# Stick-breaking attention in a hybrid block: heads paired in the array, meta keys of four heads in one tile, bonus rows parked in memory, new orders of steps

## The chip, the cores and the metric

One core of a Trainium2 chip runs the whole kernel. The metric is the device time of one execution in microseconds. The engines are TensorE (PE in the profile), VectorE (DVE), ScalarE (ACT), GpSimd (POOL) and SyncE (SP, which here only starts transfers). Each works through its own list of instructions in order and waits for the others on semaphores.

## The reference

A block on 16 learned meta tokens and 512 tokens, width 1024, float32: RMS norm, one input projection, then two branches side by side: stick-breaking attention with 8 heads of 64 and an RWKV-7 time mix with 8 heads of 64. Their outputs are projected, gated by sigmoids, added, projected again; a SwiGLU feed-forward of width 2816 follows. The attention of one head is what the change touches most:

```python
z = jnp.einsum('bhqd,bhsd->bhqs', q_blk, k).astype(jnp.float32) * (HEAD_DIM ** -0.5)
visible = jnp.arange(T)[None, :] < q_pos[:, None]
neg_log_1m_beta = jnp.where(visible, jax.nn.softplus(z), 0.0)
between = lax.cumsum(neg_log_1m_beta, axis=3, reverse=True) - neg_log_1m_beta
weights = jnp.where(visible, jnp.exp(jax.nn.log_sigmoid(z) - between), 0.0)
return jnp.einsum('bhqs,bhsd->bhqd', weights.astype(v.dtype), v)
...
bonus = jnp.sum(rh * kh * r_k.astype(f32), axis=-1, keepdims=True) * vh
y = (y + bonus.reshape(B, T, RW_WIDTH)) * g.astype(f32)
```

Only the rows of the 512 tokens leave the kernel, so only their queries are computed; keys are all 528.

## The kernel before, in words

The kernel has four stages. First the norm and 26 units of the input projection (a unit is 128 output columns; its weights are split in a high and a low half on ACT and DVE, `hi_unit` and `lo_unit`, and multiplied in three products of 8 steps each, L540). Then the **mixing stage**, with which this document deals. Then the rest of the gate units and the two branch projections, woven with the end of the time mix (`LATE`: squares, variance, gate, bonus, output). Last the output projection and the feed-forward.

In the mixing stage four kinds of work are woven into one list for each engine, written out by hand as text (`ORDER_PE`, `ORDER_ACT`, `ORDER_DVE`, `ORDER_POOL`). A token such as `a3.Q2` is a kind, a number and a step:

- `i0` to `i4`: the inverse of a triangular matrix for two chunks of 64 tokens each (steps A, L, then W, R, Y for five levels). A level goes from PE to ACT (`w`, `xt`), to PE, to DVE (`x`) and back.
- `s0` to `s8`: the recurrent state from chunk to chunk (F, RB, T0 to T2, Z, SA, OUT, S), each step handed to ACT or DVE (`z`, `sa`, `out`, `s`) and back. Both kinds are matmuls of 64x64 in the four quadrants of the array (L1389).
- `a0` to `a7`: a head of the attention. Keys lie along the partitions, so a head has four tiles of 128 keys with 512, 384, 256 and 128 visible queries and a fifth of the 16 meta keys with 512. `Q0` to `Q4` are the score products of these tiles (L1541): contraction 64, so half of the array's rows. `z0` to `z4` copy them out on ACT (L842), `m0` to `m3` mask the diagonal blocks on POOL. Softplus is `min`, `exp`, `ln(1+.)`, `max` over a row of 1792 numbers in two halves of 896. Its high and low halves (`hi`, `lo`) go through `C3` to `C0` and `C4`, products with triangles of ones that build the reversed sum in one bank (L1559, L1563), which `s3` to `s0` and `s4` subtract. `w1`, `w0`, `wm` take the exponential and `O` is the product with the values (L1576, L1578): 64 output columns, so half of the array's columns.
- `g0` to `g9`: ten gate units in four pieces of six matmuls each (L1426); `u0` is a further unit.

The score tiles of a head go to two banks by turns. The orders on ACT put the four exponentials and logarithms of a head together.

Of the kernel before, what the change touches and what calls it, by code (L numbers as in the profile page):

```python
# [28 lines left out]
F32 = mybir.dt.float32  # L29
# [26 lines left out]
N_ZERO = 3  # L56
# [10 lines left out]
K_ID, K_TRI, K_CTRI, K_BLK, K_LT, K_LE, K_IST, K_CEN, K_RST = 0, 128, 256, 384, 512, 576, 640, 704, 768  # L67
# [20 lines left out]
PIECES = 4  # L88
# [69 lines left out]
KINDS = {"i": "inv", "s": "seq", "a": "att", "g": "gate", "u": "unit"}  # L158
# [13 lines left out]
a0.Q0 a0.Q1 a0.Q2 a0.Q3 a0.Q4 i0.A i0.L a1.Q0 a1.Q1 g0.G0 i0.W1 i0.R0 a1.Q2 a1.Q3 g0.G1 g0.G2 a1.Q4 i0.Y1 a0.C3  # L172
g0.G3 a0.C2 s0.F s0.RB a0.C1 i0.W2 i0.R1 a0.C0 g1.G0 a0.C4 i0.Y2 s0.T0 s0.T1 s0.T2 g1.G1 a0.O a2.Q0 a2.Q1 a2.Q2
a2.Q3 a2.Q4 a1.C3 i0.W3 i0.R2 a1.C2 s0.Z g1.G2 a1.C1 i0.Y3 g1.G3 a1.C0 i0.W4 i0.R3 a1.C4 g2.G0 i0.Y4 g2.G1 a1.O
a3.Q0 a3.Q1 a3.Q2 a3.Q3 a2.C3 a3.Q4 i0.W5 a2.C2 i0.R4 a2.C1 g2.G2 a2.C0 i0.Y5 a2.C4 s0.SA i1.A s0.OUT s0.S i1.L
g2.G3 a2.O s1.F i1.W1 i1.R0 s1.RB a3.C3 a4.Q0 a4.Q1 a3.C2 i1.Y1 a4.Q2 a4.Q3 i1.W2 s1.T0 i1.R1 s1.T1 s1.T2 a3.C1
a4.Q4 a3.C0 i1.Y2 s1.Z1 s1.Z a3.C4 i1.W3 s1.SA i1.R2 s1.OUT1 s1.OUT s1.S i1.Y3 g3.G0 i1.W4 i1.R3 s2.F s2.RB a3.O
i1.Y4 s2.T0 s2.T1 s2.T2 g3.G1 i1.W5 i1.R4 s2.Z1 s2.Z a4.C3 g3.G2 i1.Y5 a4.C2 g3.G3 i2.A s2.SA i2.L a4.C1 s2.OUT1
s2.OUT i2.W1 s2.S i2.R0 a4.C0 g4.G0 i2.Y1 s3.F s3.RB a5.Q0 a5.Q1 i2.W2 i2.R1 s3.T1 s3.T0 s3.T2 a5.Q2 i2.Y2 a4.C4
g4.G1 g4.G2 i2.W3 i2.R2 s3.Z1 s3.Z a5.Q3 a5.Q4 i2.Y3 s3.SA g4.G3 i2.W4 i2.R3 s3.OUT1 s3.OUT s3.S a4.O i2.Y4 s4.F  # L180
s4.RB g5.G0 i2.W5 i2.R4 g5.G1 i2.Y5 s4.T1 s4.T0 s4.T2 a5.C3 i3.A i3.L a5.C2 g5.G2 i3.W1 i3.R0 s4.Z1 s4.Z a6.Q0
a6.Q1 i3.Y1 s4.SA a5.C1 i3.W2 i3.R1 s4.OUT1 s4.OUT s4.S i3.Y2 a5.C0 g5.G3 a5.C4 i3.W3 i3.R2 s5.F s5.RB a6.Q2
a6.Q3 i3.Y3 s5.T1 s5.T0 s5.T2 a6.Q4 i3.W4 i3.R3 s5.Z1 s5.Z g6.G0 g6.G1 i3.Y4 s5.SA g6.G2 i3.W5 i3.R4 s5.OUT1
s5.OUT s5.S i3.Y5 g6.G3 i4.A i4.L a5.O i4.W1 i4.R0 s6.F s6.RB g7.G0 i4.Y1 s6.T0 s6.T1 s6.T2 i4.W2 i4.R1 a6.C3
g7.G1 a6.C2 g7.G2 i4.Y2 s6.Z1 s6.Z i4.W3 i4.R2 s6.SA a7.Q0 a7.Q1 i4.Y3 a6.C1 i4.W4 i4.R3 s6.OUT1 a6.C0 i4.Y4
s6.OUT s6.S i4.W5 i4.R4 g7.G3 a6.C4 i4.Y5 s7.F a7.Q2 a7.Q3 g8.G0 a7.Q4 s7.RB g8.G1 g8.G2 g8.G3 s7.T0 s7.T1 s7.T2
g9.G0 g9.G1 s7.Z1 s7.Z a6.O s7.SA a7.C3 g9.G2 a7.C2 s7.OUT1 s7.OUT s7.S a7.C1 g9.G3 a7.C0 s8.F s8.RB a7.C4 u0.U
s8.T2 a7.O s8.Z1 s8.Z s8.SA s8.OUT1 s8.OUT
# [3 lines left out]
a0.z0 a0.z1 a0.z2 a0.z3 a0.z4 a0.exp1 a0.exp0 a1.z0 a1.z1 a0.ln1 a0.ln0 a1.z2 a1.z3 i0.xt0 i0.w1 a1.z4 g0.hi  # L192
a0.w1 i0.w2 i0.xt1 a0.w0 a0.wm a1.exp1 a1.exp0 a1.ln1 a1.ln0 a0.o a2.z0 s0.kh a2.z1 a2.z2 s0.bh a2.z3 a2.z4
i0.xt2 i0.w3 s0.z a1.w1 g1.hi a1.w0 i0.xt3 i0.w4 a2.exp1 a1.wm a2.exp0 a2.ln1 a2.ln0 a1.o a3.z0 a3.z1 a3.z2
a3.z3 a3.z4 i0.xt4 i0.w5 a2.w1 a2.w0 s0.sa a3.exp1 a3.exp0 a2.wm s0.out a3.ln1 a3.ln0 g2.hi a2.o i1.w1 i1.xt0
a4.z0 a4.z1 a4.z2 a4.z3 a3.w1 i1.w2 i1.xt1 s1.bh s1.kh a4.z4 a3.w0 s1.z s1.sa i1.w3 i1.xt2 a4.exp1 s1.out
a4.exp0 a3.wm a4.ln1 i1.xt3 i1.w4 a4.ln0 a3.o s2.bh s2.kh i1.xt4 i1.w5 s2.z a4.w1 s2.sa g3.hi s2.out i2.xt0
i2.w1 a4.w0 a5.z0 a5.z1 i2.xt1 i2.w2 s3.bh a5.z2 s3.kh a4.wm i2.xt2 i2.w3 a5.z3 s3.z a5.z4 s3.sa a5.exp1 a5.exp0
i2.xt3 i2.w4 s3.out g4.hi a5.ln1 a5.ln0 a4.o i2.w5 i2.xt4 s4.kh s4.bh a5.w1 i3.xt0 i3.w1 s4.z a6.z0 a6.z1 s4.sa
i3.xt1 i3.w2 s4.out a5.w0 g5.hi a5.wm i3.w3 i3.xt2 a6.z2 a6.z3 s5.kh s5.bh a6.z4 i3.w4 i3.xt3 a6.exp1 a6.exp0  # L200
s5.z a6.ln1 s5.sa a6.ln0 i3.xt4 i3.w5 s5.out g6.hi a5.o i4.xt0 i4.w1 s6.bh i4.xt1 i4.w2 s6.kh a6.w1 s6.z i4.w3
i4.xt2 s6.sa a7.z0 a7.z1 i4.xt3 i4.w4 a6.w0 s6.out i4.w5 i4.xt4 g7.hi a6.wm a7.z2 a7.z3 a7.z4 a7.exp1 a7.exp0
a7.ln1 s7.bh a7.ln0 s7.kh g8.hi s7.z a6.o s7.sa a7.w1 s7.out g9.hi a7.w0 a7.wm a7.o s8.z s8.sa s8.out
# [15 lines left out]
a7.lo0 g8.lo s7.decay a7.s3 a7.s2 a7.s1 s7.s g9.raw a7.s0 s8.ark s8.aak s8.arb a7.s4 g9.lo s8.v
# [22 lines left out]
def build(nc, x, meta, w_in, w_sb, w_rw, w_out, w_g, w_u, w_d, decay_up, aaa_up, gate_up,  # L242
          vecs, g_mix_pre, g_mix_post, g_ffn_pre, g_ffn_post, kf, kb, out):
    with ExitStack() as ctx:
# [34 lines left out]
        reset = consts[:, K_RST:K_RST + T]  # L279

# [14 lines left out]
        vmeta = sb("v_meta", [META, 512])  # L295
# [42 lines left out]
        cursor[0] = mix_at  # L338
# [18 lines left out]
        sp_hi = sb("softplus_hi", [P, NS], F32R)
        tri_r = sb("tri_r", [P, 2 * P], F32R)
# [92 lines left out]
        bonus_dve = sem("bonus_dve")  # L451
        tri_ok = sem("tri_ok")
# [107 lines left out]
        def y_of(p):  # L560

            return ar[:, 0, p, C:TP]


        @block.sync
        def _(sp):
# [9 lines left out]
            for dst, src in ((masks_f[:], kb), (consts[:, K_TRI:NK], kf[:, K_TRI:NK]), (lora[0:64, :], decay_up),  # L576
                             (lora[64:P, :], aaa_up), (gup[:], gate_up)):
                sp.dma_start(dst, src).then_inc(const_in, 16)
            for u in range(2, U_FFN):
                load_unit(sp, u)  # L580
                i = u - U_MIX - 4
                if 0 <= i < EARLY:
                    sp.wait_ge(mix_dve, upto(MIX_DVE, "gate", i, "raw"))
                    sp.dma_start(kept[i], gate_raw[i % 2][:]).then_inc(gate_kept[i % 2], 16)
                if u < U_OUT and MERGE[u - U_MIX][0] == "branch" and u >= U_MIX and MERGE[u - U_MIX][1] >= AHEAD:
                    j = MERGE[u - U_MIX][1]
                    if j == AHEAD:
                        for i in range(2):
# [1150 lines left out]
```

## Time and profile before

| | |
|---|---|
| time, median of 3 runs | 969.02 us (966.11 to 969.81) |
| profiled execution | 965.5 us, its span 963.7 us |
| PE busy | 921.8 us (96%) |
| DVE busy | 475.8 us (49%) |
| ACT busy | 400.8 us (42%) |
| POOL busy | 73.9 us (8%) |
| DMA | 81.17 MB, mean 84 GB/s |

The span is from the first to the last instruction; the profiled execution's own time is 1.8 us longer. Busy times are sums of instructions; matmuls are pipelined, so their busy times overlap, and what a matmul costs is read from the distance between the starts of neighbours.

### The profile page before, as it was taken

How to read it: one execution, taken by the hardware profiler on the slowest of the kernel's cores; microseconds unless marked ns; L12 is line 12 of the kernel's file. 1: busy time of each engine (PE TensorE's matmuls, PEld its weight loads, DVE VectorE, ACT ScalarE, POOL GpSimd, SP SyncE). 2: the span in 40 equal slices, each digit the busy share in tenths (PEclk: the TensorE clock that was granted, in tenths of full speed). 3: DMA queues.
4: the chain of work that ended last, by engine and by line, in shares of the span. 5: the costliest groups of instructions: out<-in, count | busy, mean ns of one | idle time of the engine just before them, and what ended most of it. 6: DMA issues, size and time to landing. Idle time of an engine off the chain costs nothing.

```text
span 963.7 us, 18924 instructions
## 1 busy us (share of the span) xinstructions
PE 921.8 (96%) x8205; PEld 739.0 (77%) x8205; DVE 475.8 (49%) x614; ACT 400.8 (42%) x576; POOL 73.9 (8%) x99
## 2 busy tenths in 40 slices
PE   4999999989999999998999996999999999999997
PEld 3999999856667677775678785888888888888886
DVE  5357876236576356362657562444444444422253
ACT  5344555356665546455444353232232232221241
POOL 1011112111111011101220000000000000000000
PEclk9999999979999999998999997999999999999999
DMA  8322212301110102121136631333332332323321
GB/s 259 103 80 81 87 50 84 88 23 35 34 35 27 42 7 69 35 66 46 45 88 220 242 84 43 87 98 98 100 96 87 90 106 87 104 93 92 105 83 70
DMA packets 108862, 81.17 MB, mean 84 GB/s; under 512 B 2878, under 2 KB 99432, under 8 KB 108792
## 3 DMA queue, kind: packets, MB, share of 16 engines
q1 hardware_dynamic: 108792, 80.13, 27.5%
q8 instruction: 57, 0.93, 0.4%
q14 instruction: 13, 0.11, 0.0%
HBM read 75.40 MB, written 4.72 MB: 83 GB/s over the span
## 4 chain that ended last, share of the span: by engine, by line
PE 92%; ACT 2%; DVE 2%; issue 2%; DMA 1%; POOL 1%; SPq 0%; POOLq 0%; DVEq 0%; ACTq 0%
PE psum L540 48%; PE psum L1624 17%; PE psum L1389 9%; PE psum L1426 6%; PE psum L1541 3%; PE psum L1578 2%; PE psum L1563 2%; PE psum L1559 1%; PE psum L1576 1%; PE psum L1310 1%; DMA x_in<-in_x 1%; ACT w_hi L525 1%; PE psum L1359 0%; PE psum L1355 0%; PE psum L1343 0%
## 5 line engine op out<-in xcount | busy, mean ns | idle before, releaser
L540 PE MATMUL psum<-h_hi,w_hi 128*128 128x512 f32 (+1 forms) x784 | 247.5, 352 | 4.8 <-DVE h_lo L998 1.7
L540 PE MATMUL psum<-h_lo,w_hi 128*128 128x512 f32 (+1 forms) x784 | 244.3, 348 | 0.0
L540 PE MATMUL psum<-h_hi,w_lo 128*128 128x512 f32 (+1 forms) x784 | 242.7, 346 | 0.0
L540 PEld LDWEIGHTS psum<-h_hi,w_hi 128*128 128x128 f32 x784 | 137.7, 190 | 27.7 <-issue 4.1
L540 PEld LDWEIGHTS psum<-h_lo,w_hi 128*128 128x128 f32 x784 | 137.0, 190 | 20.0 <-issue 1.2
L540 PEld LDWEIGHTS psum<-h_hi,w_lo 128*128 128x128 f32 x784 | 137.0, 190 | 18.7
L530 DVE TENSOR_TENSOR w_lo<-w_raw,w_hi 128x1024 fp32r<-128x1024 f32 x69 | 85.7, 1243 | 132.1 <-ACT w_hi L525 132.1
L1265 DVE TENSOR_TENSOR w_lo<-w_raw,w_hi 128x1024 fp32r<-128x1024 f32 x44 | 53.9, 1225 | 138.7 <-ACT w_hi L976 138.7
L525 ACT ACTIVATE w_hi<-w_raw 128x1024 fp32r<-128x1024 f32 x70 | 73.7, 1054 | 81.0 <-PE psum L1624 63.4
L976 ACT ACTIVATE w_hi<-w_raw 128x1024 fp32r<-128x1024 f32 x44 | 46.5, 1056 | 72.5 <-PE psum L540 72.5
L1624 PE MATMUL psum<-w_hi,act_hi 128*128 128x512 f32 x144 | 45.7, 389 | 0.0
L1624 PE MATMUL psum<-w_lo,act_hi 128*128 128x512 f32 x144 | 45.7, 389 | 0.0
L1624 PE MATMUL psum<-w_hi,act_lo 128*128 128x512 f32 x144 | 45.6, 389 | 0.0
L973 ACT ACT_TABLE_LOAD x11 | 14.1, 1283 | 54.8 <-PE psum L540 54.8
L1541 PE MATMUL psum<-qT,kT 64*128 64x512 f32 (+4 forms) x80 | 33.5, 532 | 3.3 <-DVE tri_r L1091 3.2
L1426 PE MATMUL psum<-h_hi,w_hi 128*128 128x512 f32 x80 | 34.5, 432 | 0.1
L973 ACT ACTIVATE ffn_t<-psum 128x512 f32<-128x512 f32 x22 | 13.2, 599 | 50.5 <-PE psum L540 50.4
L1112 DVE COPY_PREDICATED x_inv<-byte_masks,psum 128x512 f32<-128x512 uint8 (+1 forms) x25 | 16.9, 677 | 33.7 <-PE psum L1389 33.6
L1169 DVE TENSOR_TENSOR scores<-scores,psum 128x128 f32<-128x128 f32 (+4 forms) x40 | 20.9, 523 | 23.5 <-PE psum L1563 23.3
L1426 PE MATMUL psum<-h_lo,w_hi 128*128 128x512 f32 x80 | 32.1, 401 | 0.0
L1426 PE MATMUL psum<-h_hi,w_lo 128*128 128x512 f32 x80 | 32.1, 401 | 0.0
L1624 PEld LDWEIGHTS psum<-w_lo,act_hi 128*128 128x128 f32 x144 | 27.0, 188 | 5.7
(257 smaller groups left out, 1454.9 us busy)
## 6 DMA issues: line engine op xcount, KB each, us to landing
w_raw<-in_w_in SPq DMA_DIRECT2D x42, 512.0 KB, 3.8
w_raw<-in_w_g SPq DMA_DIRECT2D x22, 512.0 KB, 3.8
w_raw<-in_w_u SPq DMA_DIRECT2D x22, 512.0 KB, 3.8
w_raw<-in_w_d SPq DMA_DIRECT2D x22, 512.0 KB, 3.6
w_raw<-in_w_out SPq DMA_DIRECT2D x8, 512.0 KB, 5.5
kept_gates<-gate_raw SPq DMA_DIRECT2D x10, 256.0 KB, 2.3
sig_t<-kept_gates SPq DMA_DIRECT2D x10, 256.0 KB, 3.0
x_in<-in_x SPq DMA_DIRECT2D x4, 512.0 KB, 6.4
```

What stands on the lines that cost most here:

```text
L525: nc.scalar.activation(split(u)[0][:], raw[u % RAW][:], ACT.Copy).then_inc(w_hi_done, 1)
L530: nc.vector.tensor_sub(lo[:], raw[u % RAW][:], hi[:].bitcast(F32)).then_inc(w_split, 1)
L540: mm = nc.tensor.matmul(o, w[:, (w0 + i) * P:(w0 + i + 1) * P], xs[:, k, c0:c1], start=(n == 0), stop=(n == total - 1))
L973: s_.activation(ffn_t[t][:], bank(2 * t), ACT.Sigmoid).then_inc(f_sig, 1)
L976: s_.activation(w_hi[v % SPL][:], raw[v % RAW][:], ACT.Copy).then_inc(w_hi_done, 1)
L1169: v_.tensor_tensor(d, d, psum[0:rows, CBANK, SEQ - WIDTH[j]:SEQ], ALU.subtract).then_inc(mix_dve, 1)
L1265: v_.tensor_sub(w_lo[v % SPL][:], raw[v % RAW][:], w_hi[v % SPL][:].bitcast(F32)).then_inc(w_split, 1)
L1389: mm = t_.matmul(psum[rows(p, hd, moved), bnk + p // 2, o0:o0 + n], w(k, p), m(k, p), start=first, stop=last, skip_group_check=True)
L1426: mm = t_.matmul(bank(GBANK), w[:, k * P:(k + 1) * P], xs[:, k, META:T], start=(k == 0 and i == 0), stop=(k == KT - 1 and i == 2))
L1541: t_.matmul(psum[0:kn, QBANKS[j % 2], 0:WIDTH[j]], kT[lanes, hp, k0:k0 + kn], qT[lanes, hp, SEQ - WIDTH[j]:SEQ], start=True, stop=True).th ...
L1563: mm = t_.matmul(psum[0:kn, CBANK, SEQ - WIDTH[j]:SEQ], tri_r[0:kn, 0:kn], part[0:kn, OFF[j]:OFF[j] + WIDTH[j]], start=(j == 3 and part is ...
L1624: mm = t_.matmul(bank(2 * b + h), xs[:, k, P * b:P * b + P], w[:, 512 * h:512 * h + 512], start=(k == 0 and i == 0), stop=(k == n - 1 and ...
```

## The change

1. **Pairs of heads.** `a0` to `a3` are now pairs. `Q0`, `Q1`, `Q2` issue the products of both heads in turn, one on the upper and one on the lower 64 rows of the array, into a bank each; `Q2` holds the tiles of 256 and 128 queries, which share a bank. One ACT instruction `z` copies both banks. `O` issues the ten matmuls in turn for the two heads, one to the left and one to the right 64 columns. The softplus part stays by head, and is named `h0` to `h7`; its two parts are now 896 and 384 long instead of 896 and 896.
2. **Meta keys.** `m0` and `m1` hold the 16 meta keys of four heads each, at partitions 0, 32, 64 and 96 of one tile of 512 queries: two matmuls with 64 output columns each (`km` holds the keys, with zeros between), one `min`, `exp`, `ln`, `max`, `hi`, `lo` for four heads. `C4` multiplies this tile with a triangle by blocks of 32 (`K_TM`).
3. **Bonus rows.** To make room, the 1 MB of bonus rows is written to memory before the mixing stage (`kept_bonus`) and read back when `i4.x5` is done. ACT, DVE and POOL have tiles there and DVE and POOL wait for the write; POOL's addition in `LATE` waits for the read.
4. **Gate pieces.** A gate unit is two pieces of twelve matmuls (`PIECES = 2`).
5. **Orders.** All four lists are new. PE no longer waits for the copy `tri_r` ahead of the stage, only ahead of the first C.

```diff
-PIECES = 4
+PIECES = 2
...
+                if u == N_IN + 1:
+                    sp.wait_ge(bonus_dve, PAIRS)
+                    sp.dma_start(kept_bonus, bonus[:]).then_inc(bonus_kept, 16)
...
+                if i == EARLY:
+                    for k in range(2):
+                        sp.wait_ge(gate_kept[k], 16 * ((EARLY + 1 - k) // 2))
+                    sp.wait_ge(bonus_kept, 16)
+                    sp.wait_ge(mix_dve, upto(MIX_DVE, "inv", len(BATCHES) - 1, f"x{LEVELS - 1}"))
+                    sp.dma_start(bonus[:], kept_bonus).then_inc(bonus_back, 16)
...
-            pe.wait_ge(tri_ok, 1)
...
+                if kind == "att" and s[0] == "Q":
+
+                    j = int(s[1])
+                    if j == 2:
+                        if n < 2:
+                            pe.wait_ge(mix_act, upto(MIX_ACT, "meta", n, "z"))
                         else:
+                            pe.wait_ge(mix_act, upto(MIX_ACT, "att", n - 2, "o"))
+                    else:
+                        pe.wait_ge(mix_act, upto(MIX_ACT, "att", n, f"z{j + 1}"))
+                    for t in ((0,), (1,), (2, 3))[j]:
+                        k0, c0 = META + P * t, OFF[t] - OFF[j]
+                        for hr in range(2):
+                            mm = t_.matmul(psum[:, QBANKS[hr], c0:c0 + WIDTH[t]], kT[head(hr), n, k0:k0 + P],
+                                           qT[head(hr), n, SEQ - WIDTH[t]:SEQ], start=(t == j), stop=True,
+                                           skip_group_check=True)
+                    mm.then_inc(mix_pe, 1)
...
+                    for j in range(QB):
+                        for hr in range(2):
+                            v0 = (2 * n + hr) * HD
+                            mm = t_.matmul(psum[head(hr), QBANKS[1], SEQ - WIDTH[j]:SEQ], vtok[:, j, v0:v0 + HD],
+                                           zs[n % 2][:, hr, OFF[j]:OFF[j] + WIDTH[j]], start=False, stop=(j == QB - 1))
```

What the orders do is shown at three places. At the start of the mixing stage PE has, before, the five score products of head 0 one after the other (`qT,kT`, with the number of output partitions and of queries), then the first steps of the inverse (`a_r,b_t`, `b_t,a_r`):

```order
L1541 MATMUL psum<-qT,kT 128x512
L1541 MATMUL psum<-qT,kT 128x384
L1541 MATMUL psum<-qT,kT 128x256
L1541 MATMUL psum<-qT,kT 128x128
L1541 MATMUL psum<-qT,kT 16x512
L1389 MATMUL psum<-a_r,b_t 64x64 x16
L1389 MATMUL psum<-b_t,a_r 64x64 x16
L1541 MATMUL psum<-qT,kT 128x512
L1541 MATMUL psum<-qT,kT 128x384
```

and of change, where `k_meta` is the tile of meta keys:

```order
L1458 MATMUL psum<-a_r,b_t 64x64 x16
L1597 MATMUL psum<-qT,k_meta 64x512 x2
L1458 MATMUL psum<-b_t,a_r 64x64 x16
L1458 MATMUL psum<-a_r,k_t 64x128 x8
L1613 MATMUL psum<-qT,kT 128x256 x2
L1613 MATMUL psum<-qT,kT 128x128 x2
L1458 MATMUL psum<-a_r,b_t 64x64 x8
L1458 MATMUL psum<-x_inv,aab 64x64 x16
L1458 MATMUL psum<-consts,x_inv 64x64 x16
L1613 MATMUL psum<-qT,kT 128x384 x2
```

The first step of the inverse now stands ahead of all scores, and the score products come in twos. At the end of the stage PE has, before, the last steps of the recurrent state, and right behind them the variance of the time mix's output (`y_sq`):

```order
L1389 MATMUL psum<-z_st,xt_121 64x64 x8
L1389 MATMUL psum<-a_r,s_st 64x64 x6
L1389 MATMUL psum<-ark,v_tm 64x64 x4
L1389 MATMUL psum<-arb,sa_st 64x64 x4
L1389 MATMUL psum<-a_r,s_st 64x64 x2
L1389 MATMUL psum<-ark,v_tm 64x64 x4
L1389 MATMUL psum<-arb,sa_st 64x64 x4
L1591 MATMUL psum<-y_sq_157,consts 128x512
L1591 MATMUL psum<-y_sq_158,consts 128x512
L540 MATMUL psum<-h_hi,w_hi_55 128x512
```

In the change a piece of gate 9 (L1495, rows left out here) stands between `z_st` and the outputs, and unit `u0` (24 matmuls, of which the first three are shown) comes behind them, ahead of `y_sq`; before, `u0` stood eight steps earlier:

```order
L1458 MATMUL psum<-arb,sa_st 64x64 x4
L1458 MATMUL psum<-a_r,s_st 64x64 x2
L1458 MATMUL psum<-ark,v_tm 64x64 x4
L1458 MATMUL psum<-arb,sa_st 64x64 x4
L550 MATMUL psum<-h_hi,w_hi_53 128x512
L550 MATMUL psum<-h_lo,w_hi_53 128x512
L550 MATMUL psum<-h_hi,w_lo_54 128x512
```

On ACT, before, exponential and logarithm of a head follow each other in one block (here from the weights of head 0 to the logarithm of head 1), with two loads of a function table for each head:

```order
L855 ACT_TABLE_LOAD
L855 ACTIVATE scores_137<-scores_137 128x384
L815 ACTIVATE w_inv<-psum 128x512
L818 ACTIVATE xt_121<-psum 128x512
L859 ACTIVATE scores_137<-scores_137 128x896
L863 ACTIVATE scores_137<-scores_137 16x512
L847 ACTIVATE softplus<-softplus 128x896 x2
L851 ACT_TABLE_LOAD
L851 ACTIVATE softplus<-softplus 128x896 x2
```

and of change (the middle of heads 2 and 3), where the parts 384 and 896 take turns and each change from exponential to logarithm and back is a load:

```order
L881 ACTIVATE softplus<-softplus 128x384
L899 ACTIVATE scores_138<-psum 128x2x384
L885 ACT_TABLE_LOAD
L885 ACTIVATE softplus<-softplus 128x384
L863 ACTIVATE a_r<-psum 128x4x64
L846 ACTIVATE w_inv<-psum 128x512
L849 ACTIVATE xt_128<-psum 128x512
L899 ACTIVATE scores_138<-psum 128x2x384
L893 ACT_TABLE_LOAD
L893 ACTIVATE scores_139<-scores_139 128x896
L881 ACTIVATE softplus<-softplus 128x896
```

Counted over the stage, ACT's list has 17 such loads before and 35 in the change.

## Rows read from the trace of the kernel before

**Rows 1.** The page: span, and busy time of PE and ACT.

```profile
span 963.7 us, 18924 instructions
PE 921.8 (96%) x8205; PEld 739.0 (77%) x8205; DVE 475.8 (49%) x614; ACT 400.8 (42%) x576; POOL 73.9 (8%) x99
```

**Rows 2.** Busy time by stretch, with granted clock, DMA share and GB/s.

```profile
195.50:200.20 4.70, 1.51 (x5) 0.67 (x4) 1.43 (x2) 1.81 (x3) 0.00 (x0) 1.00 0.10 31
200.20:213.80 13.60, 13.55 (x143) 7.72 (x144) 4.09 (x6) 9.29 (x13) 1.75 (x6) 0.50 0.01 2
445.50:452.30 6.80, 3.80 (x5) 1.76 (x6) 0.54 (x1) 6.71 (x8) 4.38 (x1) 0.54 0.01 2
...
198.70:445.50 246.80, 242.46 (x4792) 167.76 (x4792) 132.53 (x211) 137.24 (x223) 29.73 (x52) 0.97 0.13 37
```

**Rows 3.** What PE waited for, mixing stage first, then 436 to 600.

```profile
PE psum L1541 <- DVE tri_r L1091: 3.2, 1, 3.2
...
PE psum L1591 <- ACT y_sq L881: 3.0, 1, 3.0
PE psum L1389 <- ACT sa_st L829: 0.5, 1, 0.5
PE psum L1389 <- ACT z_st L826: 0.5, 1, 0.5
```

**Rows 4.** Timeline of PE, scores of head 5: start us, length, instructions.

```profile
317.91 1.77 PE L1541 MATMUL psum<-qT,kT 64*128 64x512 f32 x4
319.61 0.69 PE L1389 MATMUL psum<-x_inv,aab 64*64 64x64 f32 x32
320.13 0.65 PE L1389 MATMUL psum<-consts,x_inv 64*64 64x64 f32 x32
...
321.40 0.70 PE L1541 MATMUL psum<-qT,kT 64*128 64x256 f32 x2
322.03 0.69 PE L1389 MATMUL psum<-w_inv,xt 64*64 64x64 f32 x32
...
328.95 1.44 PE L1541 MATMUL psum<-qT,kT 64*128 64x128 f32 x4
330.32 0.69 PE L1389 MATMUL psum<-w_inv,xt 64*64 64x64 f32 x32
```

**Rows 5.** Timeline of PE, head 3 times its values.

```profile
296.05 1.07 PE L1576 MATMUL psum<-scores,v_meta 16*64 16x512 f32 x2
297.05 2.37 PE L1578 MATMUL psum<-scores,v_tok 128*64 128x512 f32 x8
299.35 0.69 PE L1389 MATMUL psum<-w_inv,xt 64*64 64x64 f32 x32
```

**Rows 6.** ACT by group, 198 to 446: count, busy us, mean ns, idle before.

```profile
L847 ACT ACTIVATE softplus<-softplus 128x896 f32<-128x896 f32 x16 | 14.7, 946 | 2.2 <-DVE softplus L1150 2.2
L818 ACT ACTIVATE xt<-psum 128x512 f32<-128x512 f32 x20 | 11.8, 592 | 10.7 <-PE psum L1389 10.6
L851 ACT ACT_TABLE_LOAD x8 | 10.3, 1283 | 0.1
L863 ACT ACTIVATE scores<-scores 16x512 f32<-16x512 f32 x8 | 5.0, 624 | 5.7 <-DVE scores L1169 5.7
L855 ACT ACTIVATE scores<-scores 128x384 f32<-128x384 f32 x8 | 4.2, 525 | 5.4 <-DVE scores L1169 5.4
```

**Rows 7.** Timeline of PE, a gate piece alone, then the unit behind the variance.

```profile
300.67 0.50 PE L1426 MATMUL psum<-h_hi,w_hi 128*128 128x512 f32 x1
302.28 0.69 PE L1389 MATMUL psum<-x_inv,aab 64*64 64x64 f32 x32
...
448.50 3.75 PE L1591 MATMUL psum<-y_sq,consts 128*128 128x512 f32 x4 [3.04 <-ACT y_sq L881]
```

**Rows 8.** DMA issues: transfers, KB each, median us to landing.

```profile
w_raw<-in_w_in SPq DMA_DIRECT2D x42, 512.0 KB, 3.8
resid<-in_x SPq DMA_DIRECT2D x4, 512.0 KB, 9.8
```

More of the change, by code:

```diff
@@ L155 @@
 LAST_C = NC_ - 1
-KINDS = {"i": "inv", "s": "seq", "a": "att", "g": "gate", "u": "unit"}
+KINDS = {"i": "inv", "s": "seq", "a": "att", "h": "sum", "m": "meta", "g": "gate", "u": "unit"}
 def order(text):
@@ new lines, in _ @@
+                if kind == "sum":
+                    j = int(s[1])
+                    if j in (3, 2):
+                        pe.wait_ge(mix_dve, last_of(MIX_DVE, "sum", h, ("hi1", "lo1")))
+                    else:
+                        pe.wait_ge(mix_dve, last_of(MIX_DVE, "sum", h, ("hi1", "lo1", "hi0", "lo0")))
+                    if j == 3:
+                        if h:
+                            pe.wait_ge(mix_dve, upto(MIX_DVE, "sum", h - 1, "s4"))
+                        else:
+                            pe.wait_ge(tri_ok, 1)
+                    else:
+                        i = 0 if j == 4 else j + 1
+                        pe.wait_ge(mix_dve, upto(MIX_DVE, "sum", h, f"s{i}"))
+                        for part in (sp_hi, sp_lo):
+                            t_.matmul(psum[:, CBANK, SEQ - WIDTH[i]:SEQ], tri_r[:, P:2 * P],
+                                      part[:, OFF[i]:OFF[i] + WIDTH[i]], start=False, stop=False,
+                                      skip_group_check=True)
+                    if j == 4:
+                        pe.wait_ge(mix_dve, last_of(MIX_DVE, "meta", h // 4, ("hi", "lo")))
+                        for part in (spm_hi, spm_lo):
+                            mm = t_.matmul(bank(CBANK), tri_r[:, 2 * P:3 * P], part[:], start=False, stop=(part is spm_lo),
+                                           skip_group_check=True)
+                    else:
+                        for part in (sp_hi, sp_lo):
+                            mm = t_.matmul(psum[:, CBANK, SEQ - WIDTH[j]:SEQ], tri_r[:, 0:P],
+                                           part[:, OFF[j]:OFF[j] + WIDTH[j]], start=(j == 3 and part is sp_hi),
+                                           stop=False, skip_group_check=True)
+                    mm.then_inc(mix_pe, 1)
@@ L1699, in tables @@
     f[:, K_CTRI:K_CTRI + P] = row < col
+    f[:, K_TM:K_TM + P] = (row // 32 == col // 32) & (row >= col) & (row % 32 < META)
     f[:, K_BLK:K_BLK + P] = row // C == col // C
```

337 lines of the change are left out of this document (182 added, 155 removed).

## The prediction, made before the change was run

> **What bounds the kernel now.** I read the page first: PE is busy for 921.8 of 963.7 us, ACT for 400.8 [rows 1]. That share says little by itself, since busy times of pipelined matmuls overlap, so the next view is the stretches. From 198.7 to 445.5 us, the mixing stage, PE is busy for 242.5 of 246.8 us, ACT for 137.2 and DVE for 132.5 [rows 2]. Then the waits: in the whole stage PE waits 3.2 us for the copy tri_r at its start, and for about half a microsecond each at other places [rows 3]. So PE's own work sets the length of the stage, and what leaves PE's list shortens the kernel, as long as ACT and DVE keep up. Two places at its edges are different. From 195.5 to 200.2 us PE is busy for 1.5 us, and the next 13.6 us run at a granted clock of 0.50, that is at 1.2 instead of 2.4 GHz [rows 2]. Behind the last state step PE waits 3.0 us for the squares, and there too the clock of the stretch is only 0.54 [rows 2, 3].
>
> **The change, part by part.** *Scores.* In rows 4 head 5 has its tiles of 512 and 384 queries from 317.91 to 319.61 (1.70 us), that of 256 from 321.40 to 322.03 (0.63) and those of 128 queries and of the meta keys from 328.95 to 330.32 (1.37): 3.70 us a head, 29.6 us for eight [rows 4]. 896 columns in 1.70 us are 1.9 ns a column. What two products side by side on the upper and lower rows cost is not in the trace for this shape. The nearest row is the inverse: 32 matmuls of 64 columns over the four quadrants take 0.52 us (319.61 to 320.13) [rows 4]. At the rate of the value product, 3.30 us (296.05 to 299.35) for 2 x 1792 columns or 0.92 ns a column [rows 5], 32 x 64 columns one by one would be 1.9 us. So four tiles run 3.6 times as fast as one. The bounds for a pair are 1 (no gain) and 2. I take nearly 2, since that row holds both tiles with different rows and tiles with different columns of the array: a pair costs 1280 x 1.9 = 2.43 us and 0.1 us for a further break, ten microseconds for four pairs, and the meta tiles 2 x 0.97. Together 12.0, a gain of **17.6 us**; with no gain from the pairing it is 23.8, a gain of 5.8.
>
> *Values.* Eight times 3.30 us [rows 5] are 26.4; four pairs at that price 13.2, a gain of **13.2 us**, or none.
>
> The Trainium skill speaks against so full a gain: "TensorE: Matmul & The Clock Gate", Part 3, gives a measured speedup of 2.38 for three column tiles, 79% of the ideal. By that share a pair would run 1.6 times as fast as two heads, and the two gains together would be about 6 us smaller. The row of the quadrants shows 3.6 of 4, or 90%, and the trace decides.
>
> *Gate pieces.* A piece of six stands from 300.67 to 302.28, 1.61 us [rows 7]; of which I estimate 0.1 to 0.2 us for the break; 34 stretches of gate work become 20, but several of the 34 follow a C step, which leaves no break. I count **1 us**. The C steps stay what they are, C4 too: it has 512 columns before and after. The sum of PE's work is 31.8 us less.
>
> *Start of the stage.* PE no longer waits for tri_r: what it needs for i0.A is there at 195.5. The 3.2 us [rows 3] go. If PE has work there, the stretch at half clock should go as well: 13.6 us at 0.50 [rows 2] hide up to 6.8 us; PE did not fill them, so I take 6. But the new order has its own waits: the first score product needs m0.z from ACT, which is behind a weight split, and W1 needs two DVE steps behind another. I take 3 us for these. Net **6.2 us**, bounds 0 (the clock falls all the same) and 9.
>
> *End of the stage.* u0 now stands behind the last state step and covers the chain of osb and squares: the 3.0 us of waiting go [rows 3], and of the variance's 3.75 us at half clock [rows 7] and the unit after it about 2.2. The waits for z_st and sa_st, 0.5 us each [rows 3], are covered by a value product and a gate piece. Net **6.2 us**. What is late next: ACT's root of the variance now comes behind a sigmoid and a weight split; that is some 0.4 us for the branch that waits for the time mix.
>
> *ACT.* It does fewer columns: 512 take 592 ns, 896 take 946, so a column costs 0.92 ns and an instruction 0.12 us [rows 6]. Copies of scores fall from 18.0 to 12.1 us, exponentials and logarithms from 30.3 (32 of 946 ns) to 25.9 (16 of 946, 16 of 525, 4 of 512 columns), wm and o from 9.7 to 4.9: 15.1 us less. But 17 loads of 1283 ns [rows 6] become 35: 23.1 us more. ACT goes from 137.2 [rows 2] to about 145 us, in a stage of some 210: from 56 to 69%. It is denser at first: at these prices ACT's list up to s4.z sums to some 105 us, PE's up to s4.SA to some 122, over 80%. Behind each load on ACT stand the copies w, xt, z, sa, out, for which PE waits. Before, such waits came to hardly a microsecond [rows 3]. I take **7 us** of new waits, bounds 1 and 23 (each added load on the path). There is also one pair of score banks instead of two by turns, so each Q waits for the z before; orders put one to four microseconds of other work between them.
>
> *Bonus rows.* 1 MB out and in. 512 KB take 3.8 us to land, 9.8 in the slowest kind of row [rows 8], so I put 1 MB at 8 to 20 us. The write starts when the fourth bonus is done, four units (24 matmuls each) ahead of the stage, which is cover enough. The read has u0, the variance and two more units, over 15 us, before POOL wants it, and the weights queued behind it on SP are for units as late. Cost 0; if that cover were gone, the excess over it, up to 5 us.
>
> Sum: 31.8 + 6.2 + 6.2 - 7 = 37.2 us. Against the profiled execution, 965.5 us, that is 928.3. The runs before it had a median of 969.0, 3.5 more, and where the clock falls varies by microseconds: I say **930**.
>
> **Rivals.** (a) *The pairs don't run side by side.* For it: no row shows 512 columns from two tiles, and both heads' scores go to all 128 output partitions. Against it: the quadrants' row. PE's work is then only 5.8 + 1 less; with PE slower the new waits are about 2: 17 us in all, **950**. The Tiling page of the Trainium skill, "TensorEngine Tiling (Array Packing)", Gotcha 1, says that different row tiles can't access one bank at a time. The score products of a pair have a bank each and would pass; the quadrants' steps before already put two row tiles into one bank, at 3.6 of 4, so the trace doesn't agree that they must take turns.
>
> (b) *The table loads are on the path.* 18 more of 1283 ns [rows 6], each seen by PE: 23 instead of 7 us of waits, 21 us in all, **946**. For it: ACT at over 80% in the first half, an engine in strict order. Against it: 17 loads in the stage before left PE without a wait.
>
> (c) *Slower: ACT becomes the bound.* The chains go PE, ACT, PE, DVE, and such a list may not fill ACT any better than now, 137.2 of 246.8 us or 0.556 [rows 2]. Then 145 us of ACT's work need 261 us, 14 more than the stage has; less the 3.2 us of the start this is 976. It decides from 44 us of PE waits on, that is when waits eat 31.8 + 6.2 + 6.2. Against it: before, PE was the one that never waited, so 0.556 was PE's doing, not ACT's.
>
> **How the numbers follow.** Chances: my forecast 0.70 (its own range 918 to 940: below with no new waits at all and nothing lost at the start, above with 13 us of waits or the low clock kept), (b) 0.17, (a) 0.08, (c) 0.05. The range 918 to 951 holds the first three but for the ends of each. Slower by over 0.5% (about what a measurement of this kernel can tell from no change) is nearly all of (c), 0.03; within 0.5% 0.02; faster 0.95.
>
> **What would show it.** In the trace after: a pair's value product in 3.3 to 3.5 us (right) or 6.6 (rival a); the three score steps of a pair in about 2.6 us or 5; the first state steps at 195.5 and a granted clock of 1.00 from there to the end of u0; the list of PE's waits with ACT's tiles at 1 to 13 us in all (forecast) or over 20 (rival b); 35 table loads; no wait for the bonus rows; the stage, u0 at its end included, from 195.5 to about 409. What would make me wrong in the large is a wait that I have not seen in the new orders, for instance ACT's first half, where a late copy delays inverse, state and scores at once, or a fall of the clock in the thinner first microseconds.

## The result, and the profile after

The changed kernel takes **916.88 us** in the median of four runs (916.27 to 917.95), the kernel before 968.58 beside it (966.11 to 969.81): a ratio of 0.947, 95% interval 0.9449 to 0.9492. The forecast was 930, its range 918 to 951: right in direction, 13 us too slow, and the result is one microsecond under the range.

The page of the changed kernel, profiled in a run of 917.2 us: the span, busy times, and the issues of the bonus rows further down.

```profile
span 915.4 us, 18891 instructions
PE 880.7 (96%) x8209; PEld 726.0 (79%) x8209; DVE 467.0 (51%) x622; ACT 409.3 (45%) x564; POOL 65.5 (7%) x84
```

The span is 48.3 us shorter [rows 1]; PE lost 41 us of busy time, ACT gained 8.5. Busy time by stretch, with granted clock, in the columns of rows 2:

```profile
195.50:200.20 4.70, 4.70 (x106) 3.04 (x107) 2.04 (x4) 2.19 (x4) 0.00 (x0) 1.00 0.34 100
200.20:213.80 13.60, 12.66 (x351) 9.03 (x348) 8.64 (x18) 12.60 (x16) 2.88 (x6) 1.00 0.01 3
195.50:402.40 206.90, 204.13 (x4790) 156.69 (x4789) 125.71 (x221) 151.70 (x218) 24.40 (x37) 1.00 0.16 46
195.50:317.00 121.50, 119.72 (x2913) 91.12 (x2911) 82.97 (x145) 101.49 (x140) 15.90 (x28) 1.00 0.14 39
280.00:310.00 30.00, 29.64 (x698) 23.27 (x700) 21.22 (x37) 27.97 (x39) 2.23 (x3) 1.00 0.19 56
```

The first two rows are the two at the start of the stage before: where PE had 1.5 us of work in 4.7 and then 13.6 us at a clock of 0.50 [rows 2], it is now full and at 1.00. The stage, unit u0 in its end included, is over at 402.2, where the variance begins; before, the variance began at 448.5 [rows 7], 46.3 us later. The clock is 1.00 throughout (the next low stretch is 537.9 to 548.1; the kernel before had one of the same length, from 585.9). Up to 317, the prediction's first half (to about s4.SA), ACT is busy for 84% of the time, as forecast (over 80%). From 280 to 310 it is busy for 93%, and PE for 99%.

All of PE's waits that the profile lists between 196 and 460 us:

```profile
PE psum L550 <- DVE w_lo L540: 1.6, 1, 1.6
PE psum L550 <- POOL orw_lo L725: 0.6, 1, 0.6
PE psum L1458 <- issue: 0.6, 2, 0.3
PE psum L1632 <- DVE scores L1232: 0.5, 1, 0.5
PE psum L1458 <- DVE aab L1145: 0.4, 1, 0.4
```

No line names ACT. The waits for tri_r, y_sq, z_st and sa_st [rows 3] are gone, and the first two lines lie behind the stage. Timeline of PE, scores first, then the values of a pair, then the variance:

```profile
220.98 0.92 PE L1613 MATMUL psum<-qT,kT 64*128 64x384 f32 x4
221.83 0.69 PE L1458 MATMUL psum<-w_inv,xt 64*64 64x64 f32 x32
...
224.67 1.13 PE L1613 MATMUL psum<-qT,kT 64*128 64x512 f32 x4
225.73 0.46 PE L1458 MATMUL psum<-v_tm,aak 64*64 64x64 f32 x16
...
251.25 1.07 PE L1656 MATMUL psum<-meta_scores,v_meta 16*64 16x512 f32 x4
252.26 2.37 PE L1661 MATMUL psum<-scores,v_tok 128*64 128x512 f32 x16
254.56 0.64 PE L1458 MATMUL psum<-w_inv,xt 64*64 64x64 f32 x28
...
402.24 1.88 PE L1674 MATMUL psum<-y_sq,consts 128*128 128x512 f32 x4
```

The pair's values take 251.25 to 254.56, 3.31 us, twice the matmuls in the time of one head's 3.30 [rows 5]: the two heads run side by side in full. The score step of 384 columns takes 0.85 us for both heads (220.98 to 221.83), the last one, 512 columns, 1.06 us (224.67 to 225.73), where one product alone has 1.9 ns a column [rows 4]. The variance takes 1.88 us instead of 3.75 [rows 7]. ACT by group, 195.5 to 402.4 us, the costliest of its loads of a table (count, busy us, mean ns, idle before):

```profile
L885 ACT ACT_TABLE_LOAD x16 | 20.5, 1283 | 0.3
L893 ACT ACT_TABLE_LOAD x7 | 9.0, 1283 | 0.1
L889 ACT ACT_TABLE_LOAD x5 | 6.4, 1283 | 0.1
```

With smaller groups there are 36 of them there, the 35 forecast and one for a gate's sigmoid (L954), which follows the stage's own list: the 18 added loads are all there, and no wait of PE shows them. The bonus rows, from the page's DMA issues (KB each, us to landing):

```profile
kept_bonus<-bonus SPq DMA_DIRECT2D x1, 1024.0 KB, 5.9
bonus<-kept_bonus SPq DMA_DIRECT2D x1, 1024.0 KB, 4.8
```

### The profile page after: what moved, and what is told of

It is laid out like the page before. It is cut to its first block, busy times and chain, and to the rows that moved or that the text cites. A ratio compares the mean times of both kernels' runs of the same rounds, so it can differ in the third digit from the quotient of the medians.

```text
span 915.4 us, 18891 instructions
## 1 busy us (share of the span) xinstructions
PE 880.7 (96%) x8209; PEld 726.0 (79%) x8209; DVE 467.0 (51%) x622; ACT 409.3 (45%) x564; POOL 65.5 (7%) x84
## 4 chain that ended last, share of the span: by engine, by line
PE 92%; DVE 3%; ACT 2%; issue 1%; DMA 1%; SPq 0%; POOL 0%; POOLq 0%; DVEq 0%; ACTq 0%
PE psum L550 50%; PE psum L1707 17%; PE psum L1458 9%; PE psum L1495 6%; PE psum L1632 2%; PE psum L1642 1%; PE psum L1613 1%; PE psum L1661 1%; PE psum L1375 1%; DMA x_in<-in_x 1%; PE psum L1424 0%; PE psum L1408 0%; PE psum L1420 0%; PE psum L1413 0%; PE psum L1656 0%
## 5 line engine op out<-in xcount | busy, mean ns | idle before, releaser
L1013 ACT ACTIVATE ffn_t<-psum 128x512 f32<-128x512 f32 x22 | 13.2, 600 | 50.5 <-PE psum L550 50.4
L1495 PE MATMUL psum<-h_hi,w_hi 128*128 128x512 f32 x80 | 32.4, 405 | 0.0
L1495 PE MATMUL psum<-h_lo,w_hi 128*128 128x512 f32 x80 | 31.7, 396 | 0.0
L1707 PEld LDWEIGHTS psum<-w_hi,act_lo 128*128 128x128 f32 x144 | 27.0, 188 | 5.6
L1707 PEld LDWEIGHTS psum<-w_hi,act_hi 128*128 128x128 f32 x144 | 26.9, 188 | 5.7 <-DVE w_lo L540 0.2
L1495 PE MATMUL psum<-h_hi,w_lo 128*128 128x512 f32 x80 | 31.4, 393 | 0.0
L788 ACT ACTIVATE shift_in<-psum 128x528 f32<-128x528 f32 x14 | 8.6, 616 | 48.5 <-PE psum L550 46.1
```

Of the source, the lines that this page charges most:

```text
L1013: s_.activation(ffn_t[t][:], bank(2 * t), ACT.Sigmoid).then_inc(f_sig, 1)
L1495: mm = t_.matmul(bank(GBANK), w[:, k * P:(k + 1) * P], xs[:, k, META:T], start=(k == 0 and i == 0), stop=(k == KT - 1 and i == 2))
L1707: mm = t_.matmul(bank(2 * b + h), xs[:, k, P * b:P * b + P], w[:, 512 * h:512 * h + 512], start=(k == 0 and i == 0), stop=(k == n - 1 and ...
```

## The experiments

Twelve kernels were run. Each is set against the changed kernel's 916.88 us, or where it starts from the kernel before, against that kernel's median beside it. The changed kernel was not run again beside them. The kernel before was, with medians of 967.3 to 967.6 us against the 968.58 of the result, so a difference of about 1 us says nothing here.

### Are the pairs really side by side, and what is each worth?

**Values one head after the other.** In the value step of a pair the head's loop goes outside:

```diff
-                    for j in range(QB):
-                        for hr in range(2):
+                        for j in range(QB):
                             v0 = (2 * n + hr) * HD
```

> The changed kernel with one edit: O issues the five value matmuls of the first head of a pair and then the five of the second, instead of the two heads in turn. Theory (two tiles of the array run side by side only when their matmuls are neighbours in PE's list): each pair's value product goes from 3.31 to about 6.6 us, four pairs 13.2 us, so about 930 us. Rival (PE's queue lets the second head's tile run ahead whatever the order, or the gain came from elsewhere): 3.3 to 3.5 us a pair, no change from 917.

Measured: 930.31 us (930.16 to 930.70), 13.4 more. Timeline of PE in it, a pair's values:

```profile
252.12 1.07 PE L1656 MATMUL psum<-meta_scores,v_meta 16*64 16x512 f32 x2
253.12 2.37 PE L1660 MATMUL psum<-scores,v_tok 128*64 128x512 f32 x8
255.42 1.07 PE L1656 MATMUL psum<-meta_scores,v_meta 16*64 16x512 f32 x2
256.42 2.37 PE L1660 MATMUL psum<-scores,v_tok 128*64 128x512 f32 x8
```

3.30 us a head, one behind the other, with the same instructions, operands and banks. So the gain is in the neighbourhood in PE's list: as two blocks of five, the matmuls on different halves do not overlap, and alternating they do, and then the second is free. The 13.2 us of the prediction is shown.

**Scores of the heads apart.** Each score step becomes two, P for the first head and Q for the second, with the next step of the order between:

```diff
-                if kind == "att" and s[0] == "Q":
+                if kind == "att" and s[0] in "PQ":
...
-                        for hr in range(2):
+                        for hr in ("PQ".index(s[0]),):
```

> The changed kernel with one edit: the score products of the two heads of a pair are pulled apart, the next step of PE's list stands between them, so that they can't run side by side. Theory: 1280 columns of 1.9 ns, 2.4 us, a pair come on top, 9.7 us for four pairs, and a break of 0.1 us at each of 12 places, so about 928 us. Rival (what made the scores cheaper is the packed meta keys and fewer breaks, the pairing itself gives little): under 3 us more, 917 to 920.

Measured: 928.81 us (928.35 to 929.85), 11.9 more, the theory's number. The score steps of the stage sum to 21.8 us instead of 11.1, so they make 10.7 of it. In the timeline the step of 384 columns takes 0.84 us for one head (226.14 to 226.98) and 0.84 for the other (227.61 to 228.45), each as long as the step of both had been:

```profile
226.14 0.91 PE L1614 MATMUL psum<-qT,kT 64*128 64x384 f32 x2
226.98 0.69 PE L1459 MATMUL psum<-w_inv,xt 64*64 64x64 f32 x32
227.61 0.91 PE L1614 MATMUL psum<-qT,kT 64*128 64x384 f32 x2
228.45 0.50 PE L1633 MATMUL psum<-softplus_hi,tri_r 128*128 128x512 f32 x1
```

Here the two heads use the upper and lower rows of the array and all its columns, and they are side by side as fully as the values, which use different columns.

**Both apart.** The two edits above together.

> The changed kernel with both pairings undone: the scores of a pair's heads are in two steps with another step between, and the values of its heads are passed one head after the other. New orders, two gate pieces, packed meta keys and the bonus rows in memory stay. Theory: the two gains add, since PE is without waits with each alone: 916.9 + 13.4 + 11.9 = 942.2, between 940 and 944. Rival: with all passes half filled again the granted clock falls as in the kernel before, 5 to 10 us more: 947 to 952, with runs apart by some us. Second rival: with PE slower, ACT and DVE have more room and waits that each alone had are gone: 939 or less.

Measured: 941.35 us (939.97 to 941.85), 24.5 more, the theory's number; the two alone sum to 25.3. The gains add, as one expects on an engine that waits for almost nothing. Its clock in the stage:

```profile
195.50:240.00 44.50, 43.53 (x830) 29.94 (x824) 26.19 (x44) 35.09 (x47) 5.30 (x11) 1.00 0.08 22
240.00:440.00 200.00, 198.47 (x4008) 146.22 (x4009) 109.90 (x184) 126.25 (x183) 21.18 (x28) 1.00 0.17 51
```

1.00 throughout, although every score and value pass again fills half of the array. That matters below.

### How much room had ACT?

**Sixteen more table loads.** A tiny square root ahead of each ln0 and ln1 makes ACT load its table and then the logarithm's (its result is not used):

```diff
                     if s[:2] == "ln":
+                        if s[2] in "01":
+                            act.wait_ge(eps_ok, 2)
+                            if padded[0]:
+                                act.wait_ge(pad_ok, padded[0])
+                            s_.activation(small[:, 29:30], small[:, 7:8], ACT.Sqrt).then_inc(pad_ok, 1)
+                            padded[0] += 1
```

> The changed kernel with a tiny square root on one column ahead of each of the 16 logarithms of the heads on ACT, which adds a table load of 1283 ns each and some 0.2 us of work: ACT gets 24 us more, from 150 to about 174 of the stage's 206 us. Theory (what the loads take is slack of ACT as long as PE's own list is longer; the 7 us of waits that were forecast for 18 added loads were not there): under 3 us more, 917 to 920. Rival (the slack is used up, in some stretches ACT is busy for over 90% already, each load now holds up the copies behind it): 10 to 24 us more, 927 to 941.

Measured: 927.60 us (926.51 to 928.61), 10.7 more: the theory fell. ACT's share in it, 220 to 250 us, then the longest of PE's waits in the stage:

```profile
220.00:250.00 30.00, 28.54 (x652) 21.69 (x650) 19.88 (x34) 29.07 (x39) 2.72 (x5) 1.00 0.19 55
```

```profile
PE psum L1466 <- ACT sa_st L862: 2.2, 1, 2.2
PE psum L1466 <- ACT w_inv L848: 1.8, 3, 0.9
...
PE psum L1466 <- DVE v_tm L1176: 1.5, 1, 1.5
```

ACT is at 97%, and PE waits 9.7 us in the stage instead of 1.5, more than half of it for ACT, above all for its copies of the inverse and the state: the picture that the prediction had drawn for the change itself.

**Eight more.** The same, ahead of ln0 alone (`if s[2] in "0":`).

> The changed kernel with 8 more table loads on ACT, each by a tiny square root ahead of ln0 of a head (16 of them, ahead of ln0 and ln1, gave 927.6, 10.7 more). About 12 us more work on ACT. Theory: ACT had some slack, which the first loads use up: less than half of the price of sixteen, 917.5 to 921. Rival: there is no slack, and each load costs alike: 922 to 923.

Measured: 920.49 us (919.94 to 920.87), 3.6 more. PE's waits for ACT in it, within the stage:

```profile
PE psum L1664 <- ACT meta_scores L912: 1.3, 1, 1.3
PE psum L1466 <- ACT w_inv L848: 0.7, 1, 0.7
...
PE psum L1621 <- ACT meta_scores L871: 0.3, 1, 0.3
PE psum L1466 <- ACT sa_st L862: 0.3, 1, 0.3
```

ACT's busy time from 195.5 us to the variance is 151.7 us in the changed kernel, 162.7 with eight loads more and 173.5 with sixteen. So the first 11 us of added ACT work cost 3.6 us (0.3 of it), the next 11 cost 7.1 (0.7). All of the first lie ahead of ln0 and all of the next ahead of ln1, so amount and place are not told apart. In the kernel before, the same stretch was this (columns as in rows 2):

```profile
195.50:448.50 253.00, 242.51 (x4793) 167.79 (x4793) 133.96 (x213) 141.73 (x229) 30.32 (x53) 0.97 0.13 36
```

The change itself had raised ACT's work by 10 us, from 141.7 to 151.7, in 46 us less time, and no wait of PE named ACT: it stands near the point from which added work on ACT is felt.

### The gate pieces

**Four pieces again.** PIECES = 4; each of the two longer stretches is cut, with the step that followed it put between.

```diff
-PIECES = 2
+PIECES = 4
```

> The changed kernel with gate units in four pieces of six matmuls instead of two of twelve; the added cuts are filled with the neighbouring step, nothing else moves. Theory (the pieces cost a break each, and two of them gave 3.6 us by the items' times, not the 1 us that was forecast): 20 more breaks of 0.15 to 0.2 us, 3 to 4 us, so 920 to 921. Rival (breaks are free, the finer weave shortens waits): 916 to 917.

Measured: 921.63 us (921.18 to 921.91), 4.8 more, a little over the theory. Twenty stretches of gate work became forty, and the 4.8 us are 0.24 for each. That is not the price of a break alone: PE also waits 2.7 us in this stage instead of 1.5, and the gate stretches themselves, each from its start to the next step's, sum to 61.7 us instead of 58.3, 0.17 us for each added one. That is the 0.1 to 0.2 us of the prediction.

**Whole units.** The first piece of each unit moves to where the second stands, so a unit is one stretch of 24 matmuls.

> The changed kernel with each gate unit in one stretch of 24 matmuls, at the place of its second piece. Theory (PE's own work sets the stage, and a break costs 0.15 to 0.2 us): 10 breaks fewer, 1.5 to 2 us less, 915. Rival (a stretch of 5.6 us holds up the chains of inverse, state and scores, so PE waits afterwards): 920 or more.

Measured: 931.32 us (930.62 to 936.13), 14.4 more; the rival holds. The longest of PE's waits in its stage:

```profile
PE psum L1632 <- DVE scores L1232: 3.6, 4, 1.6
PE psum L1458 <- DVE v_tm L1168: 2.3, 3, 1.0
PE psum L1458 <- DVE s_st L1176: 1.6, 2, 1.3
```

Fewer breaks are not worth it: with the fill in ten lumps of 5.6 us, PE waits 12.8 us in all (1.5 in the changed kernel), most of it for chains that the pieces had covered. They are 11.3 us longer, of the 14.4; the gate stretches are 1.2 us shorter, and where the other 4 us went was not read. The pieces are worth more as filler than as time saved. Of the three sizes, two pieces were the best in this order; orders written for the other two were not tried.

### The start and the end of the stage

**The wait put back.** PE waits for tri_r ahead of the stage, in the changed kernel:

```diff
+            pe.wait_ge(tri_ok, 1)
             for kind, n, s in ORDER_PE:
```

> The changed kernel with PE's wait for the copy tri_r put back ahead of the mixing stage. Theory (the idle stretch at the start brings the low clock): PE waits about 3 us, then a stretch at granted clock 0.50 follows, 5 to 6 us more: 925 to 926. Rival (the low clock before came from the thin work of head 0's scores, not from the wait): 3 us more and no low clock, 920.

Measured: 920.33 us (919.90 to 921.94), 3.4 more. Busy time by stretch in its profile:

```profile
196.70:200.00 3.30, 0.05 (x4) 0.05 (x3) 1.50 (x2) 1.54 (x2) 0.00 (x0) 1.00 0.14 43
201.30:204.60 3.30, 3.30 (x54) 2.28 (x54) 1.44 (x3) 0.60 (x1) 0.00 (x0) 0.50 0.03 7
204.60:214.00 9.40, 9.40 (x224) 6.38 (x220) 4.48 (x10) 8.48 (x12) 2.92 (x6) 1.00 0.01 3
```

The median is the rival's number, the profile is what neither expected: the idle 3.3 us bring a low clock of 3.3 us behind them, not of 13.6 as before [rows 2]. PE's waits in the stage are 4.6 us instead of 1.5, and the half clock costs 1.7: 4.8, the difference of the spans (920.2 and 915.4). The profiled run was the slowest of the four (921.9 us, the others 919.9 to 920.5), so whether the low stretch comes in every run is open.

**The wait taken away from the kernel before.** PE waits for tri_r only in the first C step, where it is used.

> The kernel before with one edit: PE waits for tri_r ahead of its first use, a0.C3, and no longer ahead of the stage. Theory: the wait of 3.2 us goes and with it the 13.6 us at granted clock 0.50, worth about 6: 8 to 9 us less, 960. Rival (head 0's five scores with one bank each wait for ACT anyway, so the idle time only moves and the clock still falls): 2 to 3 us less, 966.

Measured: 959.98 us (956.43 to 963.47) against 967.60 of the kernel before beside it, ratio 0.9896 (0.9842 to 0.9951), 7.6 less. That is near the theory's number. But the profile says that the low clock went elsewhere:

```profile
195.50:228.20 32.70, 31.96 (x428) 19.77 (x429) 20.81 (x31) 25.16 (x38) 6.03 (x11) 1.00 0.10 30
228.20:238.60 10.40, 10.40 (x122) 7.45 (x126) 3.33 (x7) 4.25 (x8) 1.93 (x4) 0.52 0.01 2
443.20:450.60 7.40, 5.56 (x9) 3.12 (x10) 2.05 (x2) 7.34 (x9) 4.52 (x1) 0.54 0.00 0
```

PE had been busy for 32.0 of 32.7 us when the clock fell, just behind 228.2, in the middle of the scores of head 2, that followed the values of head 0 at once (221.9 to 229.7). Two of the four runs took 956.4 and 957.1 us at a mean clock of 0.990, two 962.8 and 963.5 at 0.983 and 0.978. The row is worth 5 us, so this fall may be what parts the two groups; only one run was profiled, and that is not shown.

**u0 last in the kernel before.** PE's order alone, u0.U from the place ahead of s8.T2 to the end.

> The kernel before with one edit: u0 moved from ahead of s8.T2 to the end of PE's list. Theory: it covers the 3.0 us of waiting for the squares, and the clock doesn't fall behind them (2.2 us), at the price of a longer wait for a7.O's inputs and the branch's time-mix half: 4 to 5 us less, 964. Rival (the wait only moves, to a7.O or to the branch): within 1 us of 968.6.

Measured, in ten runs: 964.50 us (960.90 to 967.33) against 967.60, ratio 0.9963 (0.9939 to 0.9986), 3.1 less (by the interval 1.4 to 5.9), under the theory's 4 to 5. In its profile the wait for the squares and the half clock behind it are gone, 5.2 us, and there is a new wait of 1.0 us for head 7's last scores (L863), which u0 had covered; u0 moved over seven steps, one less than said above. The waits for z_st and sa_st stay.

**Both edits in the kernel before.**

> The kernel before with both edits: tri_r waited for at its first use, u0 last. Theory (the two edges are independent): 12 to 14 us less, 955, so that 38 to 39 of the change's 51.7 us are left for pairs, meta keys and pieces. Rival: less than 6 us together, 963 or more, and the edges explain little.

Measured: 957.18 us (951.71 to 960.69), 10.4 less by the medians; 7.6 and 3.1 add. That is between the theory's 12 to 14 and the rival's 6. The ratio is 0.9859 (0.9808 to 0.9909), which would be 13.6 us less, 8.8 to 18.6: with four runs over 9 us the edges are known to some microseconds only. Two low stretches are still in its profile, 229.4 to 239.8 and 430.2 to 437.8.

**Full passes between the half ones.** From the kernel before without its early wait; two gate pieces, g1.G2 and g1.G3, moved on PE alone:

```diff
-a0.O a2.Q0 a2.Q1 a2.Q2 a2.Q3 a2.Q4
+a0.O g1.G2 a2.Q0 a2.Q1 a2.Q2 g1.G3 a2.Q3 a2.Q4
```

> The kernel before without its early wait for tri_r (959.98 us, range 956.43 to 963.47), and two pieces of gate unit 1, whose matmuls fill all rows and columns of the array, moved forward on PE alone: one ahead of the scores of head 2 and one in their middle. Without them, in that kernel's profile, the values of head 0 and the scores of head 2 lay side by side in the program (222.0 to 229.6 us, all of them passes that use half of the array or less), and the granted clock fell to 0.50 from 228.2 to 238.6. Theory: the clock falls in long runs of half filled passes though the engine has no gap in them, so with full passes between there is no fall there, 5 us less: median 955 to 957, and all runs in that group. Rival: the fall has nothing to do with what lies at that place; it comes at the same or another place in about half of the runs, median 958 to 961. Second rival: the moved pieces come before their operands, and PE waits for them; that would be in the waits as a wait at L1426.

Measured: 959.23 us (956.95 to 961.97, six runs), the rival's number. No wait at L1426 is in its profile, so the second rival is out. Stretches of its profile:

```profile
195.50:439.30 243.80, 236.99 (x4793) 164.51 (x4792) 133.89 (x213) 139.69 (x227) 29.83 (x52) 1.00 0.13 38
439.30:446.20 6.90, 5.46 (x9) 3.05 (x10) 1.94 (x2) 6.84 (x9) 4.52 (x1) 0.51 0.00 0
```

In the profiled run the fall at 228 is gone, and that run is 4 us shorter than the one of the kernel that it starts from (958.6 to 962.8). Yet the median did not move, and the kernel with both pairings undone runs half filled passes through the whole stage at 1.00. That long runs of half filled passes make the clock fall is not shown. Six runs are too few to say whether the times of 963 us are gone for good.

## Why the prediction was off

Point by point, in the order of its sum. Where two durations of PE's list are compared, they are the times from a step's start to the next step's start, summed over the stage of either trace.

- **Scores, 17.6 us: right in kind, 1.9 too high.** A pair's three steps take 0.85, 0.85 and 1.06 us, 2.76 instead of 2.53, since each step has its own break; the meta steps 1.01. All eight heads now take 13.1 us instead of the 12.0 forecast. Before they took 28.8, not 29.6, with the half clock at the start taken off, so the gain is 15.7. The pairing's part, by undoing it, is 10.7 in the score steps and 11.9 in the median; most of the rest is the packed meta keys, eight steps of about 0.97 us [rows 4] that became two.
- **Values, 13.2: right.** 13.24 us for four pairs; 13.4 by experiment. Rival (a) is refuted by both, and by the scores. The speedup by which the Trainium skill ("TensorE: Matmul & The Clock Gate", Part 3) would have made the gains 6 us smaller is 2.38 for three column tiles. Its share of the ideal does not carry over to two: here two column tiles gave 3.31 us against 6.6, a factor of 2.0. The same skill's warning on row tiles ("TensorEngine Tiling (Array Packing)", Gotcha 1) did not bite the scores, which have a bank each.
- **Gate pieces, 1: too low by 1.1.** The gate stretches take 58.3 us instead of 61.8, but 1.4 of these 3.5 is the half clock on the first piece, which the start of the stage has already. At full clock 2.1 are left for fourteen stretches fewer, 0.15 each: the price of a break was right, and too much was taken off for stretches behind a C step. The experiment with four pieces cost 4.8, some of it new waits.
- **Start of the stage, 6.2: too low by 2.3.** The wait's 3.2 and the half clock's 6.8 both went. Of the 3 us for new waits, 1.5 are there (aab 0.4, the scores' split 0.5, 0.6 without a releaser). The reason given was half right: the idle time accounts for 3.3 + 1.7 us in the changed kernel, and in the kernel before the low stretch moved on to 228 us when the wait was taken away.
- **End of the stage, 6.2: right.** No wait for the squares, the variance at full clock, and the waits for z_st and sa_st covered. In the kernel before, u0's place alone gave 3.1: there it laid bare a wait of 1.0 and left the waits for z_st and sa_st, which the new orders don't have.
- **ACT's new waits, 7: this is the step that failed.** It was 0. The load itself was forecast well: 69% of the stage (it is 151.7 of 206.9 us, 73%) and over 80% in the first half (84%). The prediction took it as a reason for waits, and put a number between the bounds 1 and 23 without a row for it. What the runs showed in its place: the orders put the copies far enough ahead that even at 93% no PE wait names ACT, and the room ends a little beyond, at 0.3 us lost per microsecond added, then 0.7. Rival (b) had 23 us of waits; even 22 us more of ACT's work than the change has cost only 10.7. Rival (c) is refuted by the same rows.
- **The 1.7 us from the profiled run to the median.** They came of the kernel before, whose thirteen runs in one set spread over 9 us, from 964.8 to 973.9, at mean clocks from 0.983 to 0.969. The changed kernel's median is its profiled time less 0.3, and its four runs spread over 1.7.
- **Small waits of the kernel before, not in the forecast.** Beside those in rows 3, PE waited 1.7 us without a releaser and 0.2 for k_t. The forecast left them in; the 1.5 us counted at the start are all that the change has.
- **Bonus rows, 0: right.** They land in 5.9 and 4.8 us; nothing waits for them.

7 for ACT, 2.3 for the start, 1.1 for the pieces and 1.9 for the small waits, less 1.9 for the scores, are 10.4 of the 11.1 us between 928.3 and the profiled 917.2; the other 2 are the median. Read from the two profiled runs, the gains are 15.7 for scores, 13.1 for values, 2.1 for pieces, 8.5 for the start, 6.2 for the end and 1.9 for small waits: 47.5 of the 48.3 us between the spans.

The experiments account for most of the 51.7 us between the medians: 24.5 for both pairings, 4.8 for the pieces, 10.4 for start and end in the kernel before, and by the traces some 5.7 for the packed meta keys, 45.4 in all. The remaining 6 were not isolated by a run, and the 10.4 is uncertain by as much. The traces say where they can lie: start and end are 14.7 us between the two profiled runs. The profiles of all four variants of the kernel before still have low stretches in this stage, worth 3.4 to 8.5 us by their length, while of the variants of the changed kernel only the one with the wait put back has one. What sets them off was not found, and moving work at one such place did not move the median.

## What to carry to other kernels

Where one engine's list hardly waits, its own instructions set the time, and the clock they run at: here the second of two passes on different halves of the array cost nothing if the two alternated in the list, and the two such gains added. Another engine's rising load is no wait until a row names it; before putting a number on it, ask how many microseconds of other work the order leaves between that engine's copy and its reader, and if it can be tried, pad that engine by a known amount to see where its room ends. Cut filler into pieces by what chains they must cover: in this order one size down cost 5 us, one size up 14. And take the half clock off before two durations are compared, or it is counted twice.

## What the runs showed of the hardware that was not expected

- Two column tiles, and two row tiles, of f32 passes overlap in full: 3.31 us for two heads' values against 3.30 for one, 0.84 us for 384 score columns of one head and 0.85 for both heads. They did so alternating in the list; in series the values take 6.6.
- ACT at 28.0 of 30 us made PE wait for nothing; 11 us more on it in the stage cost 3.6, 22 us 10.7.
- The granted clock fell from 1.00 to 0.50 for some 10 us right behind a stretch in which PE had been busy for 32.0 of 32.7 us, so an idle gap is not the only thing ahead of a fall; the runs of that kernel lie in two groups 5 us apart. After an idle stretch of 3.2 to 3.3 us the low stretch was 3.3 us long in one order and 13.6 in another.
